# Two-block transformer kernel on one core: the first modulation stage taken by shift and scale pairs

## The reference, cut to what matters

```
cond = silu(c)                                   # c: 1024 numbers
mod = cond @ ada_w[0] + ada_b[0]                 # 6 x 1024
sh1, sc1, g1, sh2, sc2, g2 = split(mod, 6)
h = rms_norm(x, norm_mix[0]) * (1 + sc1) + sh1
q, k, v = split(h @ a_w_in[0], 3)                # 1024 -> 3072
```

## Time and profile before

| | us |
|---|---|
| median of three runs | 1058.52 |
| the profiled execution's own time | 1061.51 |
| its span in the trace | 1059.8 |
| PE busy | 1026.2 (97%) |
| DVE busy | 765.8 (72%) |
| ACT busy | 550.5 (52%) |
| POOL busy | 101.4 (10%) |

### The profile page before, as it was taken

How to read it: one execution, slowest core, us unless ns; L and a number is a source line. 1 busy time by engine, 2 the same in 40 slices (tenths; PEclk the granted TensorE clock), 3 DMA queues, 4 the chain that set the end, 5 groups by cost and what they waited for, 6 DMA issues and landing times.

```text
span 1059.8 us, 17084 instructions
## 1 busy us (share of the span) xinstructions
PE 1026.2 (97%) x6050; PEld 899.0 (85%) x6050; DVE 765.8 (72%) x1368; ACT 550.5 (52%) x918; POOL 101.4 (10%) x160
## 2 busy tenths in 40 slices
PE   6999989999999999999999999999999999899996
PEld 6887878899999988889999899999988888788885
DVE  5788787987888677777768755655568786587863
ACT  1457755534544456644344435444346676566662
POOL 0041101000000010011000000000004021030210
PEclk9699999899999989999999999999999999999998
DMA  9966755688787638857686464566427540175501
GB/s 370 334 228 215 256 190 208 217 291 299 266 276 275 232 129 311 284 211 240 217 275 209 156 189 158 191 202 201 168 100 239 193 163 23 60 264 183 169 11 41
DMA packets 57197, 218.46 MB, mean 206 GB/s; under 512 B 6420, under 2 KB 11540, under 8 KB 51000
## 3 DMA queue, kind: packets, MB, share of 16 engines
q1 hardware_dynamic: 48368, 169.24, 46.6%
q0 software_dynamic: 6048, 43.52, 11.4%
q10 hardware_dynamic: 2728, 5.00, 1.5%
HBM read 216.67 MB, written 1.06 MB: 205 GB/s over the span
## 4 chain that ended last, share of the span: by engine, by line
PE 88%; DVE 4%; ACT 3%; DMA 2%; issue 1%; POOL 0%; SPq 0%; ACTq 0%; DVEq 0%
PE ps L1743 26%; PE ps L1744 25%; PE ps L1745 25%; PE ps L1847 2%; PE ps L2225 2%; PE ps L1812 1%; PE ps L1802 1%; PE ps L1792 1%; DVE w_lo L1008 1%; PE ps L2115 1%; PE ps L2273 1%; DMA arena<-in_adastream 1%; PE ps L1835 1%; ACT w_hi L554 1%; DMA raw<-in_wstream 1%
## 5 line engine op out<-in xcount | busy, mean ns | idle before, releaser
L1008 DVE TENSOR_TENSOR w_lo<-raw,w_hi 128x1024 fp32r<-128x1024 f32 (+1 forms) x312 | 355.5, 1180 | 64.5 <-ACT w_hi L554 57.7
L554 ACT ACTIVATE w_hi<-raw 128x1024 fp32r<-128x1024 f32 (+1 forms) x312 | 307.1, 1020 | 134.4 <-DMA raw<-in_wstream 96.2
L1743 PE MATMUL ps<-h_hi,w_hi 128*128 128x256 f32 x704 | 201.8, 287 | 1.0 <-DVE h_lo L1087 0.8
L1744 PE MATMUL ps<-h_lo,w_hi 128*128 128x256 f32 x704 | 200.4, 285 | 0.0
L1745 PE MATMUL ps<-h_hi,w_lo 128*128 128x256 f32 x704 | 200.3, 285 | 0.0
L1743 PE MATMUL ps<-w_hi,h_hi 128*128 128x512 f32 (+1 forms) x480 | 190.4, 397 | 4.7 <-DVE h_lo L1087 3.0
L1745 PE MATMUL ps<-w_hi,h_lo 128*128 128x512 f32 (+1 forms) x480 | 184.5, 384 | 0.0
L1744 PE MATMUL ps<-w_lo,h_hi 128*128 128x512 f32 (+1 forms) x480 | 184.5, 384 | 0.0
L1743 PEld LDWEIGHTS ps<-h_hi,w_hi 128*128 128x128 f32 x704 | 136.3, 194 | 4.1 <-issue 2.6
L1743 PE MATMUL ps<-w_hi,a_hi 128*128 128x512 f32 x352 | 137.4, 390 | 1.5 <-DVE a_lo L1461 1.5
L1744 PE MATMUL ps<-w_lo,a_hi 128*128 128x512 f32 x352 | 137.2, 390 | 0.0
(11 more groups left out here) (221 smaller groups left out, 1331.1 us busy)
## 6 DMA issues: line engine op xcount, KB each, us to landing
raw<-in_wstream SPq DMA_DIRECT2D x296, 512.0 KB, 5.2
ada_raw<-in_adastream POOLq DMA_DIRECT2D x40, 1024.0 KB, 5.1
ada_raw<-in_adastream SPq DMA_DIRECT2D x4, 1024.0 KB, 9.3
arena<-in_adastream SPq DMA_DIRECT2D x4, 1024.0 KB, 10.7
row<-in_gate_rows ACTq DMA_DIRECT2D x5, 512.0 KB, 4.1
raw<-in_wsmall SPq DMA_DIRECT2D x16, 128.0 KB, 2.2
row<-in_params POOLq DMA_DIRECT2D x2, 769.0 KB, 5.3
x<-in_x SPq DMA_DIRECT2D x1, 1024.0 KB, 9.6
```

Source lines behind the costliest of these rows:

```text
L554: act.activation(w_hi[:, c % SPLIT, at], raw[:, n, 0:width // 2], ACT.Copy)\
L1008: nc.vector.tensor_tensor(w_lo[:, c % SPLIT, at], raw[:, (2 * c + h) % RAW, 0:width // 2], w_hi[:, c % SPLIT, at].bitcast(F32), ALU.subtract)\
L1743: nc.tensor.matmul(dst, sh, mh, start=start, stop=False)
L1744: nc.tensor.matmul(dst, sh, ml, start=False, stop=False)
```

## The change

DVE takes the four shift chunks 0 to 3, PE the four scale chunks 4 to 7; of chunk 7 DVE sums the lower four tiles and PE adds that sum by a product with ones. The chunks are loaded as 0, 4, 1, 5, 2, 6, 3, 7, each into a buffer of its own, so that SP waits for none of them; two of them lie in `raw`, and the first weights wait for the first sum and the first product. After each pair of chunks the shift and scale of two feature tiles are formed (`first_modulation`), ACT writes both `h_hi` and `f` of that pair (`first_operand_hi`, four instructions where two were), DVE the low part. The first projection runs by pairs too: two feature tiles over both token blocks, and then the next two. PE runs 24 idle products at its start, 12 after the first pair, 4 before the last product, and one after every four products of `first_product`. Their operand is a tile of zeros that DVE writes first. The diff, cut to its core:

```diff
+FIRST_ORDER = (0, 4, 1, 5, 2, 6, 3, 7)
         first_ada = [v.rearrange("p (k n) -> p k n", n=AW) for v in (
-            spare[:, 0:CW], part(8192, CW), spare[:, CW:2 * CW], part(4096, CW), part(6144, CW),
-            spare[:, 0:CW], part(8192, CW), spare[:, CW:2 * CW])]
+            raw[:, 0:2].rearrange("p a b -> p (a b)"), spare[:, 0:CW], part(8192, CW),
+            part(4096, CW), raw[:, 2:4].rearrange("p a b -> p (a b)"), spare[:, CW:2 * CW],
+            part(6144, CW), ada_acc[:, 6:14].rearrange("p a b -> p (a b)"))]
...
-            first(7)
+            for n in range(4, FIRST_ADA):
+                first(n)
+            sp.wait_ge(s_ada, 1)
+            sp.wait_ge(s_first_used, 1)
...
             ada_load(adastream[8], 0, 4)
+            pool.wait_ge(s_first_used, 2)
             ada_load(adastream[9], 1, 8)
...
+            def first_operand_hi(pr):
+                act.wait_ge(s_modp, pr + 1)
+                act.wait_ge(s_xT, pr + 1)
+                for dst in (h_hi, f):
+                    for b in range(2):
+                        k = 2 * pr + b
+                        last = act.activation(dst[:, k, :], ps[:, 4 + pr, b * S:(b + 1) * S],
+                                              ACT.Identity, scale=mod_scale[:, 0, k:k + 1],
+                                              bias=mod_shift[:, 0, k:k + 1])
+                last.then_inc(s_f, 1)
+            first_operand_hi(0)
             act.wait_ge(s_t5c, 1)
             act.dma_start(dist, t5_row).then_inc(s_dist, 16)
-            split(0)
-            modulate(0, mod_scale[:, 0], mod_shift[:, 0])
+            first_operand_hi(1)
+            hi_part(0, 0, CW)
+            first_operand_hi(2)
+            hi_part(0, 1, CW)
+            first_operand_hi(3)
...
             first_sum(0)
+            first_modulation(0)
             norm_x(0)
-            first_sum(2)
+            first_sum(1)
             dve.wait_ge(s_t5ps, 1)
             nc.vector.tensor_copy(t5_row, ps[0:4, 1, :]).then_inc(s_t5c, 1)
-            first_sum(4)
-            first_sum(5)
-            first_sum(7)
-            dve.sem_inc(s_ada, len(FIRST_PE))
-            split(0)
-            modulation(0, 0)
-            operand(0)
+            first_operand_lo(0)
+            first_sum(2)
+            first_modulation(1)
+            first_operand_lo(1)
+            first_sum(3)
+            first_half_sum(7, 4)
+            lo_part(0, 0, CW)
+            first_modulation(2)
+            first_operand_lo(2)
+            lo_part(0, 1, CW)
+            first_modulation(3)
+            dve.sem_inc(s_mod, 1)
+            dve.sem_inc(s_ada, FIRST_ADA - 5)
+            first_operand_lo(3)
             split(1)
             split(2)
...
+            def first_product(a, shared=None):
+                pe.wait_ge(s_first[a], 16)
+                bank = 2 + a % 2
+                for b in range(2):
+                    v = slice(b * P, (b + 1) * P)
+                    dst = ps[:, bank, 2 * a + b:2 * a + b + 1]
+                    for k in range(4 if shared else 0, KT):
+                        last = nc.tensor.matmul(dst, first_ada[a][:, k, v], cond[:, k:k + 1], ...)
+                        if k == 3:
+                            keep_warm_first(1)
+                    if shared:
+                        pe.wait_ge(s_ada, shared)
+                        last = nc.tensor.matmul(dst, ada_acc[:, (a + ADA_AT) % ADA_KEPT, v],
+                                                ones[:, 0:1], start=False, stop=True)
+                    keep_warm_first(1)
+                last.then_inc(s_first_used, 1)
+            pe.wait_ge(s_fill, 1)
+            keep_warm_first(24)
+            pe.wait_ge(s_cond, 1)
+            pe.wait_ge(s_set, 4)
+            first_product(4)
+            pe.wait_ge(s_ada, 1)
+            first_columns(0)
+            keep_warm_first(12)
             pe.wait_ge(s_in, 16)
             transpose_x(0)
...
-            columns(0, 0, [b for b in range(16) if b // 2 not in FIRST_PE])
-            keep_warm(2, 8)
-            pe.wait_ge(s_mod, 1)
+            first_product(5)
+            pe.wait_ge(s_ada, 2)
+            first_columns(1)
+            pe.wait_ge(s_modp, 1)
+            first_product(6)
+            pe.wait_ge(s_ada, 3)
+            first_columns(2)
+            pe.wait_ge(s_modp, 2)
+            keep_warm_first(4)
+            first_product(7, 5)
+            first_columns(3)
+            pe.wait_ge(s_t5c, 1)
...
+            for half in range(2):
+                for j in range(2):
+                    pe.wait_ge(s_wlo, 2 * half + j + 1)
+                    operand_in(0, 4 * half + 2 * j)
+                    for t in range(TT):
+                        for n in (2 * j, 2 * j + 1):
+                            k = 4 * half + n
+                            last = matmul3(ps[:, t, :], tokens(k, t), weights(half, 512, n),
+                                           k == 0, k == KT - 1)
```

More of the change, by code:

```diff
@@ L51 @@
 FIRST_ADA = 8
-FIRST_PE = (1, 3, 6)
+FIRST_ORDER = (0, 4, 1, 5, 2, 6, 3, 7)
 C_QKV = 0
@@ L360, in load, with first @@
                         .then_inc(s_raw[n % RAW], 16)
[L362 to L366, removed]
+            def first(n):
+                a = FIRST_ORDER[n]
                 sp.dma_start(first_ada[a].rearrange("p k n -> p (k n)"), adastream[a])\
@@ L1149, in head_sums @@
                                         ALU.add).then_inc(s_qss, 1)
+            own.inc(nc.vector.memset(ada_odd[:], 0.0))
+            own.wait()
+            for b in range(2):
+                last = nc.vector.tensor_copy(a_hi[:, 0, b], ada_odd[:])
+            last.then_inc(s_fill, 1)
             dve.wait_ge(s_cols, 16)
@@ L1156, in _, with first_half_sum @@
             dve.wait_ge(s_cond, 1)
+            dve.wait_ge(s_fill, 1)
             def first_sum(a):
                 dve.wait_ge(s_first[a], 16)
-                ada_sum(first_ada[a], ada_acc[:, (a + ADA_AT) % ADA_KEPT, :],
-                        a - len([b for b in FIRST_PE if b < a]) or None)
+                ada_sum(first_ada[a], ada_acc[:, (a + ADA_AT) % ADA_KEPT, :], a or None)
+            def first_half_sum(a, count):
+                dve.wait_ge(s_first[a], 16)
+                dst = ada_acc[:, (a + ADA_AT) % ADA_KEPT, :]
+                ada_sum(first_ada[a], dst, count, range(4))
+                own.wait()
+                nc.vector.tensor_tensor(dst, dst, ada_odd[:], ALU.add).then_inc(s_ada, 1)
@@ new lines, in first_modulation @@
+            def first_modulation(pr):
+                dve.wait_ge(s_modps, pr + 1)
+                bank, n, v = 2 + pr % 2, 2 * pr, slice(2 * pr, 2 * pr + 2)
+                nc.vector.tensor_tensor(mod_shift[:, 0, v], ps[:, bank, n:n + 2],
+                                        cols[:, COL_ADA + n:COL_ADA + n + 2], ALU.add)
+                own.inc(nc.vector.tensor_tensor(mod_scale[:, 0, v], ps[:, bank, 8 + n:10 + n],
+                                                cols[:, COL_ADA + 8 + n:COL_ADA + 10 + n],
+                                                ALU.add))
+                own.wait()
+                nc.vector.scalar_tensor_tensor(mod_scale[:, 0, v], mod_scale[:, 0, v], 1.0,
+                                               cols[:, COL_NORM + n:COL_NORM + n + 2],
+                                               ALU.add, ALU.mult).then_inc(s_modp, 1)
@@ L1837, in keep_warm_wide @@
                                      stop=True)
-            pe.wait_ge(s_cond, 1)
[L1842 to L1851, removed]
@@ L1853, in _, with keep_warm_first @@
-            first_product(FIRST_PE[0])
+            def keep_warm_first(n):
+                for _ in range(n):
+                    nc.tensor.matmul(ps[:, 0, :], a_hi[:, 0, 0, 0:P],
+                                     a_hi[:, 0].rearrange("p a b -> p (a b)"), start=True,
+                                     stop=True)
+            def first_product(a, shared=None):
+                pe.wait_ge(s_first[a], 16)
+                bank = 2 + a % 2
+                for b in range(2):
+                    v = slice(b * P, (b + 1) * P)
+                    dst = ps[:, bank, 2 * a + b:2 * a + b + 1]
+                    for k in range(4 if shared else 0, KT):
+                        last = nc.tensor.matmul(dst, first_ada[a][:, k, v], cond[:, k:k + 1],
+                                                start=k == (4 if shared else 0),
+                                                stop=k == KT - 1 and not shared)
+                        if k == 3:
[6 more added lines that the diff above has]
+                last.then_inc(s_first_used, 1)
@@ new lines, in first_columns @@
+            def first_columns(a):
+                bank = 2 + a % 2
+                for b in range(2):
+                    last = nc.tensor.matmul(
+                        ps[:, bank, 2 * a + b:2 * a + b + 1],
+                        ada_acc[:, (a + ADA_AT) % ADA_KEPT, b * P:(b + 1) * P], ones[:, 0:1],
+                        start=True, stop=True)
```

(12 more changed lines are left out.)

18 lines of the change are left out of this document (8 added, 10 removed).

## The result

The changed kernel takes 1066.39 us (median of 14 runs, 1062.08 to 1069.66), the kernel before, on the same chip, 1059.56 (14 runs, 1057.27 to 1067.93). The ratio is 1.0056, 95% interval 1.0039 to 1.0073: slower, by some 6 us. The forecast was 1063.5 us, +5.0 on the 1058.5 it started from. The profiled execution took 1067.44 us (span 1065.8) against 1061.51.

What follows compares the result with a forecast made beforehand. PE was taken as the bound: its first projection would end at 58.8 against 53.0 us (+5.8), less 0.8 for DVE idle, so 1058.5 + 5.0 = 1063.5 us; range 1055.3 to 1066.5.

Steps and rivals of the forecast that it cites:

- The level: PE's clock, 1.2 or 2.4 GHz: one idle product per eight records was forecast to lose the higher during the scale products.
- product 5: PE's product of scale chunk 5: begins at the higher clock and loses it, 5 us, ending at 27.7 us.
- the level holds: Rival, chance 0.33: PE keeps the higher clock through the scale products, DVE then bounds; -2.4 us, 1056.1 us.
- The sum: PE's times added from its first idle products to the first projection's end: 58.8 against 53.0 us, +5.8 us.
- transposes and table: PE's 16 transposes (2.5 us) and small table product (0.5 us) after the twelve idle products, done at 22.7 us.
- product 6: PE's product of scale chunk 6, 32 records and four idle products, all at the lower clock: 8.7 us.
- half chunk: PE's product for half of chunk 7, 16 records, four of the shared sum, two idle products: 5.2 us.
- The mark: ACT takes up the first projection's last bank, released by PE: 53.01 us before, forecast 58.8 us.
- PE is last: In the first projection, DVE and ACT would allow the third quarter at 53.3, the fourth at 56.0 us; PE ends later.
- The 0.8 us won back: Taken off +5.8 us because DVE's idle of 1.47 and 0.93 us shortly behind might be partly won back.
- POOL's added wait: 0: POOL's new wait lies ahead of chunk 9, which DVE reads after 60 us, so it costs 0.
- clock lost in the products: The forecast case itself, chance 0.53: PE loses the higher clock in the scale products and is late by 5 us.

## Why the prediction was right

**The level.** The forecast was that one idle product per eight records would lose the level as it had at 373 us. It fell at 13.8 us (forecast 14.3) and at 27.4 (in product 5, as forecast), and was back at 20.6 us, just ahead of the transposes (0.73 in the window at 20 us). The rival "the level holds" did not come. The Trainium skill (TensorE: Matmul & The Clock Gate, section "Why this matters for your kernels") gives as the way to avoid drops in the middle of a kernel that no long idle gaps are left between bursts of products. That was not enough here: PE was busy 1.00 of 1.00 us in every window from 5 to 60 us, and the clock fell.

**The sum.** The terms stand beside the measured ones: transposes and table done at 22.7 us, measured 23.5; product 5 with its idle products 5 us, measured 5.3 (23.50 to 28.82); product 6 8.7 us, measured 8.7 (29.47 to 38.21); four idle products 1.7, measured 1.9; half chunk 5.2, measured 5.1; projection from 46.0, measured 46.39. The start of the projection owes something to luck: the table was done 0.8 us late, and the three pairs of columns behind it, taken at 0.9 us each, took 0.65. The mark was put at 58.8 us and came at 59.88. Of the 1.1 us, 0.4 is the later start; the term that was short is the low beginning of the projection. Eight products in 3.7 us were assumed, as before from 40.1 us, but the level came back only in the window at 51 us: about eleven ran low, three more at 0.2 us each, 0.6 us. The time of 1066.39 us lies only 0.1 us inside the upper end of the stated range (1066.5). The forecast of +5.0 us was short by these 1.1 us and by the 0.8 us taken off for DVE, and the kernel before was 1.0 us slower in these runs than in the three that the forecast started from.

**"PE is last."** Right, and by the margins given: DVE waits 3.09 us for the columns before pair 3, and neither waiting by halves nor the earlier loads moved the changed kernel. Pair 3 was ready at 49.7 us (forecast 49.1).

**The 0.8 us won back** was wrong. At 70.56 us the transposes are as late as the mark was (+6.9). DVE's idle ahead of it was not there to be used: DVE is late for its own reason. Its low parts of the second chunk free the slots for the fourth, they follow pair 3, and pair 3 follows PE's columns. The prediction said that these weights would not make the loss up; it should then have taken nothing off.

**"POOL's added wait: 0"** held for the changed kernel, but not for the reason given. The prediction looked only at who reads chunk 9 (after 60 us) and not at whom the load meets. Both loads went out late (36.28 and 47.53 us, before 28.59 and 31.95). Without the 14 the second was issued at 41.47 us, ahead of the fourth weight chunk's halves (45.13 and 46.26), and ACT got these 6.5 and 6.7 us after their issue, where it had been 3.8 and 5.0 in the kernel before and was 4.0 and 6.0 with the loads early. In the changed kernel the same lateness stands behind PE's, and removing it gave 0 (ratio 1.0051 against 1.0056).

**What the loss is.** Forecast as "clock lost in the products", it is measured as the price of the 14 idle products: 6.1 us over the four products, 0.44 us each, and 0.8 us more at the start of the projection. Six of the 14 ran at the higher level and cost about as much as the eight at the lower. The level was equally lost without them, and the kernel before had lived with it as well (6 records in the window at 24 us). The sum had the 14 in it, so its size was right; the sentence that names the cause was not. A lost clock is no difference between the two kernels; products that buy no clock are.

## What to carry to other kernels

An idle product between narrow ones costs PE about 0.4 us at either level (1.13 against 0.73 us for eight records at the higher, 2.14 against 1.74 at the lower), although wide products in a row start every 0.23 us at the higher. Place it where PE would wait anyway (here the 24 gained 3.1 us), or in one block ahead of work that it makes faster by more than the block costs (the 12: 2.1 us gained). Between pieces of work that are ready it is a loss (the 4 cost 1.9 us, the 14 cost 6.1), unless a trace shows that its density holds the level and that the records saved are worth more than the filling. And when an edit makes one engine earlier, look 20 us on for the engine that is full there: here PE's earliest transposes (62.86 us) ended in a wait of 2.3 us for DVE, with the clock lost again behind it. The kernel before had PE and DVE meet at 79.1 to 79.2 us, so there PE alone had nothing to gain.

## What the runs showed of the hardware

- PE at 1.00 busy lost the higher level with 0, 1 and 3 idle 128x512 products per eight one-column records; with 0 and 1 within 1.0 us of each other (12.8 and 13.8 us, 26.4 and 27.4 us), with 3 after a much longer stretch (29.5 us).
- Behind the loss at 13 us, all twelve 128x512 products of zeros ran at the lower pace (5.2 to 5.5 us), and the level rose only at their end (20.6 us) or in the transposes behind them (0.72 in the window at 19 us without the 14). Zeros as operands do count: the 24 at the start, with nothing ahead of them, went from four to six starts per us at 6 to 7 us.
- Transposes do not bring the level back each time: in the kernel before the records behind them and the table product ran high (11 in the window at 22 us), in the kernel without idle products they ran low (6.99 us for 32).
- The granted clock of a trace is not always the pace. In the kernel without idle products every window from 5 to 72 us reads 1.00, while 32 records take 6.96 us (the lower pace) and the first products of the projection start every 0.43 us. The row of the window at 12 us, with 6 records in it:

```profile
12.00:13.00 1.00, 1.00 (x6) 1.00 (x6) 0.00 (x0) 1.00 (x3) 0.09 (x1) 1.00 0.95 401
```
